# mLSTM stage of a two-layer trunk: the negated maxima are spread over the partitions by DMA from DRAM, the numerators get four banks, and VectorE's work is ordered two units and one unit ahead

## The reference, cut to what matters

```
b = cumsum(log_sigmoid(fg));  log_d = b[j] - b[s] + ig[s]  (s <= j, else -inf)
m_row = maximum(max(log_d, axis=-1), log_inter)
s   = (q k^T) * exp(log_d - m_row)
num = s @ v;   den = sum(s)
h   = num / maximum(abs(den), exp(-m_row));    y = h_forward + h_backward
```

## Time and profile before

| | |
|---|---|
| median of three runs | 3169.11 us (3162.59 to 3169.40) |
| the profiled execution | 3163.79 us, span of its core 3162.1 us |
| mean granted PE clock over the span | 0.908 of full speed |
| gate rows and columns of the mLSTM stage | 505.0 to 523.6 us of the span |
| the loop over eight units | 523.6 to 626.1 us, 102.5 us |
| in the loop | PE busy 71.27 us, DVE 56.43, ACT 18.23, POOL none; DMA share 0.00; granted clock 0.84 |
| after the loop, to the end of the stage | 626.1 to 654.2 us |

### The profile page before, as it was taken

One profiled execution on the slowest core, in us unless ns is written; L12 is line 12 of the kernel. 1 busy time (PEld: TensorE's weight loads), 2 busy tenths in 40 slices (PEclk: granted clock), 3 DMA queues, 4 the chain that ended last, 5 costly groups with the idle time before them and its releaser, 6 DMA issues. The chain is left out here.

```text
span 3162.1 us, 41427 instructions
## 1 busy us (share of the span) xinstructions
PE 2478.9 (78%) x18136; PEld 1212.7 (38%) x18136; DVE 824.3 (26%) x1765; ACT 477.7 (15%) x960; POOL 327.7 (10%) x487
## 2 busy tenths in 40 slices
PE   4489995627487788888888697799996788888887
PEld 0134442414144333333333344688884322222222
DVE  1200503545502211111101601567652210000001
ACT  0100002222102000000001201444441100000001
POOL 0000000025101000000000500535340000000000
PEclk9889997869798899999999798799998899898999
DMA  9731110000023699999997223333222899999997
GB/s 377 295 109 66 68 53 0 1 1 1 0 80 115 272 421 408 400 414 418 421 395 298 65 73 130 60 69 58 57 45 76 347 416 414 408 404 414 390 420 299
DMA packets 192005, 692.38 MB, mean 219 GB/s; under 512 B 88952, under 2 KB 124320, under 8 KB 142288
## 3 DMA queue, kind: packets, MB, share of 16 engines
q1 hardware_dynamic: 190704, 689.24, 55.8%
q10 hardware_dynamic: 1120, 0.48, 0.1%
HBM read 675.82 MB, written 13.84 MB: 218 GB/s over the span
## 5 line engine op out<-in xcount | busy, mean ns | idle before, releaser
L1424 PE MATMUL bank<-moe_w,moe_xT 128*64 128x512 f32 (+3 forms) x3072 | 628.0, 564 | 67.2 <-DMA moe_w<-in_exp_w 64.5
L1448 PE MATMUL bank<-moe_w,moe_hidT 128*64 128x512 f32 (+1 forms) x1408 | 382.6, 699 | 128.1 <-DMA moe_w<-in_exp_w 116.5
L1424 PEld LDWEIGHTS bank<-moe_w,moe_xT 128*64 128x64 f32 (+1 forms) x3072 | 197.3, 125 | 503.7 <-issue 400.7
L1448 PEld LDWEIGHTS bank<-moe_w,moe_hidT 128*64 128x64 f32 (+1 forms) x1408 | 110.5, 139 | 363.2 <-issue 218.0
L1516 DVE TENSOR_TENSOR moe_silu<-bank,moe_silu 64x512 f32<-64x512 f32 (+3 forms) x96 | 56.5, 639 | 658.1 <-ACT moe_silu L1479 658.1
L1529 DVE COPY moe_rows<-bank 32x512 f32<-32x512 f32 x96 | 65.9, 686 | 536.4 <-PE bank L1448 535.5
L1479 ACT ACTIVATE moe_silu<-bank 64x512 f32<-64x512 f32 (+3 forms) x96 | 46.2, 546 | 1032.0 <-PE bank L1424 1032.0
L402 PE MATMUL bank<-w_slab,mixT 128*128 128x512 f32 x384 | 166.2, 593 | 1.8 <-PE bank L402 1.5
L1558 POOL TENSOR_TENSOR moe_xn<-moe_xn,moe_w 128x1024 f32<-128x1024 f32 x6 | 18.1, 3019 | 1431.2 <-ACT moe_w L1495 1431.2
L399 PE MATMUL bank<-mixT,w_slab 128*128 128x512 f32 x320 | 141.1, 602 | 10.6 <-DMA w_slab<-in_ab_w_in 9.5
L1678 PE MATMUL bank<-mixture,rw_slab 128*128 128x512 f32 (+1 forms) x384 | 143.6, 527 | 4.5 <-PE bank L1678 3.7
(11 more groups left out here) (468 smaller groups left out, 2997.7 us busy)
## 6 DMA issues: line engine op xcount, KB each, us to landing
moe_w<-in_exp_w SPq DMA_DIRECT2D x256, 1408.0 KB, 13.5
moe_w<-in_exp_w SPq DMA_DIRECT2D x64, 2048.0 KB, 18.8
ada_slab<-in_ada_w SPq DMA_DIRECT2D x32, 1536.0 KB, 12.8
moe_w<-in_exp_w SPq DMA_DIRECT2D x32, 1536.0 KB, 7.1
w_slab<-in_ab_w_in SPq DMA_DIRECT2D x11, 2048.0 KB, 7.8
wo_slab<-in_ab_w_out SPq DMA_DIRECT2D x16, 512.0 KB, 3.5
x_inv_and_t<-x_blocks SPq DMA_DIRECT2D x32, 256.0 KB, 5.0
rw_slab<-in_rw_wk SPq DMA_DIRECT2D x4, 1024.0 KB, 7.3
```

The lines of the kernel that those rows point to most:

```text
L1424: mm = pe.matmul(g.ps[k][64 * m:64 * m + M, 0:hi - lo], xg[:, i % 2, j, c, :], wa[:, sl, m, r, lo:hi], start=(c == 0), stop=(c == DC - 1))
L1448: mm = pe.matmul(g.ps[5 + m][64 * m:64 * m + M, :], hidt[:, c, :], wb[:, sl, c - lo, 512 * m:512 * m + 512], start=(c == 0), stop=(c == FC ...
```

## The change

`negw` and the spread matmuls go. `negm` is a tile of its own, of 36 partitions. When it is ready, SP writes it to a DRAM tensor `ml_negm_rows`, waits for that, and then issues eight DMAs, one for each unit, that each read one row of 2 KB and write it to all 128 partitions of `negb[:, u, :]` (256 KB a piece), with one semaphore each. D and E read `negb` in SBUF in place of banks 4 and 5. The numerators use the four banks 4 to 7, one for each tile jt, and tile jt of a unit waits for F of the same tile of the unit before. DVE's order becomes D(0), D(1), W(0), and then for each u: D(u+2), W(u+1), F(u).

```diff
-        negw = sb("ml_negm", [P, T])
-        negm = negw[0:36, :]
+        negm, negb = sb("ml_negm", [36, T]), sb("ml_negm_spread", [P, 2 * ML_H, T])
+        rows = nc.dram_tensor("ml_negm_rows", [36, T], F32).ap()
...
+                sp.wait_ge(s_rows, 1)
+                sp.dma_start(rows, negm[:, :]).then_inc(s_kept, 16)
+                sp.wait_ge(s_kept, 16)
+                for u in range(2 * ML_H):
+                    r = ROW(u % 2, u // 2)
+                    sp.dma_start(negb[:, u, :], rows[r:r + 1, :].broadcast_to([P, T])).then_inc(s_bc[u], 16)
...
                 def diagonal(u):
                     h, d = u // 2, u % 2
-                    dve.wait_ge(s_bc, u + 1)
+                    dve.wait_ge(s_bc[u], 16)
...
-                        ins = dve.scalar_tensor_tensor(diag[:, d, st, :], g.ps[4 + d][:, st * P:(st + 1) * P],
+                        ins = dve.scalar_tensor_tensor(diag[:, d, st, :], negb[:, u, st * P:(st + 1) * P],
...
-                        ps = g.ps[6 + jt % 2]
+                        ps = g.ps[4 + jt]
...
                 diagonal(0)
+                diagonal(1)
+                weigh(0)
                 for u in range(2 * ML_H):
-                    if u:
-                        finish(u - 1)
+                    if u + 2 < 2 * ML_H:
+                        diagonal(u + 2)
                     if u + 1 < 2 * ML_H:
-                        diagonal(u + 1)
-                    weigh(u)
-                finish(2 * ML_H - 1)
+                        weigh(u + 1)
+                    finish(u)
...
-                            g.act.do(act.activation(e[:, d, st, lo * P:hi * P], g.ps[4 + d][:, lo * P:hi * P], ACT.Exp,
+                            g.act.do(act.activation(e[:, d, st, lo * P:hi * P], negb[:, u, lo * P:hi * P], ACT.Exp,
...
-                def spread(u):
-                    h, d = u // 2, u % 2
-                    if u >= 2:
-                        pe.wait_ge(s_exp, u - 1)
-                    r = ROW(d, h)
-                    pe.matmul(g.ps[4 + d][:, :], g.ident[:, r:r + 1].broadcast_to([P, P]), negw[:, :], start=True, stop=True).then_inc(s_bc, 1)
...
-                        if n >= 2:
-                            pe.wait_ge(s_out, n - 1)
+                        if n >= NT:
+                            pe.wait_ge(s_out, n - NT + 1)
...
-                spread(0)
                 scores(0)
                 for u in range(2 * ML_H):
-                    if u + 1 < 2 * ML_H:
-                        spread(u + 1)
```

More of the change, by code:

```diff
@@ L528, in stage_mlstm @@
         s_bias, s_zero, s_lin, s_ln, s_rows, s_cols, s_colsc = (g.sem(n) for n in ("gate_bias", "bias_zeroed", "forget_linear", "forget_log", "gate_rows", "gate_cols", "gate_cols_copied"))
-        s_enm, s_score, s_bc, s_diag, s_exp, s_w, s_num, s_out = (g.sem(n) for n in ("enm", "scores", "m_spread", "diag_ready", "exp_ready", "weights_ready", "num_ready", "num_out"))
+        s_enm, s_score, s_diag, s_exp, s_w, s_num, s_out = (g.sem(n) for n in ("enm", "scores", "diag_ready", "exp_ready", "weights_ready", "num_ready", "num_out"))
+        s_kept = g.sem("ml_rows_kept")
+        s_bc = [g.sem(f"m_spread{u}") for u in range(2 * ML_H)]
         s_sq, s_rt, s_sig, s_y, s_tp, s_ev = (g.sem(n) for n in ("ml_squares", "ml_root", "ml_sigmoid", "ml_y", "ml_transposed", "ml_evicted"))
@@ L563, in _ @@
                 g.dve.do(dve.memset(b[:, :], 0.0))
-                g.dve.do(dve.memset(negw[:, :], 0.0))
+                g.dve.do(dve.memset(negm[:, :], 0.0))
                 g.dve.join(dve)
@@ L698, in numerators @@
                         n = NT * u + jt
-                        if n >= 2:
-                            pe.wait_ge(s_out, n - 1)
+                        if n >= NT:
+                            pe.wait_ge(s_out, n - NT + 1)
                         for st in SEES[d][jt]:
-                            mm = pe.matmul(g.ps[6 + jt % 2][:, 0:ML_DV + 1], e[:, d, st, jt * P:(jt + 1) * P], g.v[:, st, h, :],
+                            mm = pe.matmul(g.ps[4 + jt][:, 0:ML_DV + 1], e[:, d, st, jt * P:(jt + 1) * P], g.v[:, st, h, :],
                                            start=(st == SEES[d][jt][0]), stop=(st == SEES[d][jt][-1]))
                         mm.then_inc(s_num, 1)
-                spread(0)
                 scores(0)
                 for u in range(2 * ML_H):
-                    if u + 1 < 2 * ML_H:
-                        spread(u + 1)
                     if u % 2 == 1 and u + 1 < 2 * ML_H:
```

## The result

The changed kernel takes 3141.43 us (median of six runs, 3136.67 to 3147.88); the kernel before, six runs in all with those made beside it, 3175.30 us (3162.59 to 3188.66). The ratio is 0.9891, 95% interval 0.9858 to 0.9923: 34.6 us less, between 24 and 45. The profiled execution took 3136.67 us, its span is 3134.7 us, 27.4 under the span before.

What follows compares the result with a forecast made beforehand. PE and DVE waiting for each other bound the eight-unit loop; DVE's 57.1 us plus 1.0 of stalls ends it 37 us earlier. So 3163.8 becomes 3126.8, or 3132.1 by the median; middle 3129.5, range 3122 to 3141 us.

Steps and rivals of the forecast that it cites:

- The bound: Eight-unit loop, 102.5 us: PE and DVE wait for each other, 36.9 us for numerators; after the change DVE bounds it.
- The sum: Loop from W(0) at 530.6: 57.1 us of DVE's work plus 1.0 of stalls, ending at 588.7, 37 us earlier.
- The stalls left inside: Loop's slow start: waits for F(0)'s last tile 0.2 us, scores 0.4, and some hand-offs of 0.1; 1.0 in all.
- The time: Whole kernel: 3129.5 us, the middle of 3126.8 and 3132.1; 8 in 10 for 3122 to 3141.
- (a): PE's clock in the loop doesn't hold: gain only 10 to 32 us; chance 0.11 with (b), low throughout 0.04.
- (b): DVE in the loop waits for late E at odd units, 10 us come back, gain 27; chance 0.11 with (a).
- cover: Time by which E is ready ahead of W: about 4 us after even units, 2 to 3 after odd, N(1) only just.
- (c): Rows spread by DMA arrive late, 12.4 us for each 256 KB, making the kernel slower; chance 0.02.
- (d): F(u) on DVE still comes ahead of its numerators; possible only by PE's lateness, as in (a); no own chance.
- What cost nothing: PE's eight dropped spreads, 0.9 us each, worth nothing; D and E reading SBUF put at 0, -0.5 to +0.5.
- the ring: Loop on PE and DVE: F(u) stands directly behind W(u) and needs what W(u) just released; a pair takes 24.7 us.

Runs made afterwards that it cites:

- the first four experiments: Changed kernel's parts, against the kernel before: rows by DMA only, 1.0012; with four banks, 0.9986; new order only, 0.9952; rows by DMA with new order, 0.9952.
- e5: Changed kernel with every matmul of the scores done twice; stage 69.27 us against 65.80 for the change.
- e8: Changed kernel with D one unit ahead instead of two, order D(u+1), W(u+1), F(u); stage 84.46 us against 65.80.
- e7: Changed kernel with the eight row DMAs issued in reverse, unit 0's row last; stage 72.04 us against 65.80.
- e4: Kernel before with only the rows spread by DMA, old order and two banks; stage 104.52 us against 104.17, ratio 1.0012.
- e6: Changed kernel with F done for two tiles at a time; stage 61.83 us against 65.80, ratio to the kernel before 0.9885.

## Why the prediction was right

**The bound.** It said that the loop was bound by waits of PE and DVE for each other, and that the order with four banks ends them. The waits for numerators went from 36.9 us to none (0.3 us of idle time); the four combinations of order and banks put -4.8, -17.5 and -38.4 us on the banks, the order and both. That is shown; how much of it the faster clock carries is not.

**The sum.** From `negm` to the first square it had 8.7 us to W(0) and 58.1 from there, 66.8 in all; measured 9.3 and 56.5, 65.8. W(0) came 0.6 later, since the first row took 3.9 us from its issue (and the hand-off), not 3.1, and E(0), which now reads SBUF, took 0.1 longer; the write took 1.8, not 2.0. From W(0) on, 57.1 of DVE's work was a little too much: a W was taken as lasting till PE's start, 2.04 and 2.11, but F's first operation shows a start just ahead of that of W's memset, 1.92 and 1.98 from W's start (540.56 to 542.48, 547.80 to 549.78). That is 1.0 us over eight units. The stalls left inside, 1.0 by the forecast, were about 0.4, of which 0.3 for scores.

**The time.** 37 us were forecast, 38.4 measured in the stage and 34.6 (24 to 45) in whole times. The time itself, 3129.5, was 12 us low, and the median of 3141.43 stands 0.4 past the range's upper edge of 3141, at it when rounded. The step that failed is the base: the sum started from the middle of 3163.8 and 3169.1, but the later runs of the kernel before took 3181 to 3189, and their median is now 3175.3. In 31 runs beside the first four experiments it was 3163.53 to 3188.71. Of the 12 us, 8.9 are this base (3175.3 in place of 3166.4) and 3.1 the gain (33.9 between the medians in place of 37). The scatter of a kernel's own runs should have stood in the range as a term of its own, and three runs that lay 7 us apart did not show it.

In the profiled execution 11 us of the stage's gain don't appear in the span (27.4). They were not lost in the mLSTM stage or the two after it: SP's first DMA of the state-space stage is 39.7 us earlier, and its last slab of the output projection 39.7 us too. Between the last read of the second layer's key pairs and its output projection the executions of ten kernels took 141.0 to 148.6 us, before being the lowest and the change the highest, and from there to the last DMAs they took 751.4 to 758.9, before 752.1 and the change 758.9, with no order by what was edited in either stretch. These are 7.6 and 6.8 us; I take this as scatter, and what moves it from run to run was not looked into.

**The rivals.** (a) PE's clock held: 1.00 from 535.8 to 582.0, though PE had gaps of 0.8 and 0.9 us before the scores and up to 1.2 before numerators. By the rule of the Trainium skill's page "TensorE: Matmul & The Clock Gate", section "A second HAM failure mode: psum-queue depth-cycling", taken from another kernel, the clock would have gone up and down here; this trace shows 1.00 throughout that stretch and disagrees. With e5 PE was busier still and the clock the same. (b) E was never late after the start: 0.4 us of cover before W(3), 2.6 before W(5) and 1.5 before W(7), where about 0 had been foreseen for W(3) and 2 to 3 for the others; e8 shows what it costs when the cover is gone, 20.0 us in eight units, at most 2.6 in one. (c) The rows came in time: all eight in 3.8 to 5.5 us each from issue to landing, and none but the first was waited for. e7 shows the price of lateness, a little more than one for one (6.2 us for 5.4), and that the margin for the first row is nil. (d) Didn't occur.

**What cost nothing.** The transport of the rows alone: +0.4 us (e4). SP's nine issues took 4.6 us and nobody waited for SP. D's operations read SBUF at 348 ns where they had read a bank at 344 ns; E's 28 wide operations read SBUF more slowly than a bank (below), 0.1 us more in a unit, hidden behind DVE in all units but the first.

## What to carry to other kernels

When two engines are each half idle in a loop, lay out one period of it and look for the step that stands directly behind the one that releases its input. Moving other work of the same engine in between pays the whole wait, but only if there are buffers for what the other engine makes meanwhile: of 38.7 us, the banks alone gave 5.2 here and the order alone 17.9. Once the ring is open, a sum over the fuller engine's own steps gives the time to within a microsecond or two, and the next gains are in that engine's steps, as far as the other engine still has time to spare (in e6, 4.0 of 7.4 us).

## What the runs showed of the hardware that I had not expected

- A wide exponential reads SBUF more slowly than a bank. By ACT's groups the 128x256 form is 494 ns from SBUF, against 462 from a bank in the kernel before; 128x128 is 388 against 361, and 128x384 601 against 562. It doesn't hang on the order: the mean of the 28 wide operations is 462 ns in e4, with the old order and rows in SBUF, against 433 before.

```profile
L660 ACT ACTIVATE ml_weights<-ml_negm_spread,ml_gcol 128x256 f32<-128x256 f32 x12 | 5.9, 494 | 0.0
L660 ACT ACTIVATE ml_weights<-ml_negm_spread,ml_gcol 128x128 f32<-128x128 f32 x12 | 4.7, 388 | 0.0
L660 ACT ACTIVATE ml_weights<-ml_negm_spread,ml_gcol 128x384 f32<-128x384 f32 x4 | 2.4, 601 | 0.0
```

- Eight 256 KB spreads of one 2 KB run each, issued within 4.3 us, landed 3.8 to 5.5 us after their issue, against 2.9 to 5.0 for 256 KB in distinct long runs (`k_pair`, kernel before). In e7 the last of them, which D(0) waited for, took about 5.4 us.
- PE kept 2.4 GHz with gaps of about 1 us in every unit at 87% busy (40.29 of 46.20 us), where it was granted 0.50 to 0.59 after gaps of 3 to 4 us in the kernel before.
